# Two hybrid layers after a routed block: the first four column groups of each layer multiplied before the root is known, and four stores at the end

## The reference, cut to what matters

```python
def rmsnorm(x, w):
    xf = x.astype(jnp.float32)
    y = xf * lax.rsqrt(jnp.mean(xf * xf, axis=-1, keepdims=True) + EPS)
    return (y * w.astype(jnp.float32)).astype(x.dtype)
...
    h = rmsnorm(h_res, n_mix_pre)
    proj = jnp.einsum('bld,de->ble', h, w_in)
    (a_b, a_c, a_x, s_z, s_xbc, s_dt, r_q, r_k, r_v, r_g,
     sb_q, sb_k, sb_v, gate_logits) = jnp.split(proj, IN_SPLITS_2, axis=-1)
...
    mix = jnp.einsum('bld,de->ble', merged, w_out)
    h_res = h_res + rmsnorm(mix, n_mix_post)
    f = jnp.einsum('bld,df->blf', rmsnorm(h_res, n_ffn_pre), w_ffn_in)
    f_gate, f_up = jnp.split(f, 2, axis=-1)
    f = jnp.einsum('blf,fd->bld', jax.nn.silu(f_gate) * f_up, w_ffn_out)
    return h_res + rmsnorm(f, n_ffn_post)
```

## Time and profile before

| | us |
|---|---|
| median of three runs | 2256.66 (2256.37 to 2258.24) |
| the profiled execution | 2259.11 |
| its span in the profile | 2257.3 |
| TensorE busy | 2177.1 (96%) |
| VectorE busy | 1524.3 (68%) |
| ScalarE busy | 1186.3 (53%) |
| mean granted TensorE clock | 0.983 of full speed |

### The profile page before, as it was taken

The page is one execution under the profiler, slowest core; times in us unless marked ns, Lnnn a source line. Parts: engine busy times, 40 slices in busy tenths (PEclk is TensorE's granted clock), DMA queues, the critical chain, the costliest instruction groups (busy, mean ns, idle before and its releaser), DMA issues.

```text
span 2257.3 us, 39324 instructions
## 1 busy us (share of the span) xinstructions
PE 2177.1 (96%) x17046; PEld 2043.1 (91%) x17046; DVE 1524.3 (68%) x1923; ACT 1186.3 (53%) x1419; POOL 0.2 (0%) x4
## 2 busy tenths in 40 slices
PE   7988999999899999999998999899999999999997
PEld 6878888888899899999998999799899999998997
DVE  8977899999686675444555764786675445556763
ACT  4554677777452644436755444453644446745442
POOL 0000000000000000000000000000000000000000
PEclk9998999999999999999999999999999999999999
DMA  8473899998344444344343444345444444344552
GB/s 346 175 267 118 315 370 374 373 368 324 153 167 172 169 160 167 139 148 150 113 143 136 170 167 151 150 168 176 165 167 169 150 151 148 113 154 156 185 187 85
DMA packets 64317, 432.14 MB, mean 191 GB/s; under 512 B 7792, under 2 KB 11024, under 8 KB 13712
## 3 DMA queue, kind: packets, MB, share of 16 engines
q1 hardware_dynamic: 64144, 429.61, 51.8%
HBM read 428.50 MB, written 1.08 MB: 190 GB/s over the span
## 4 chain that ended last, share of the span: by engine, by line
PE 91%; DVE 5%; ACT 2%; issue 1%; DMA 1%; SPq 0%; ACTq 0%; DVEq 0%
PE banks L1870 64%; PE banks L1888 10%; PE quad L1888 5%; PE quad L555 1%; PE single L568 1%; PE quad L519 1%; PE quad L455 1%; DVE area_y L2386 1%; PE quad L558 1%; PE quad L503 1%; DVE slot_rounded L1005 1%; PE quad L543 1%; DVE slot_rounded L2420 1%; ACT area_y_rounded L661 1%; PE single L1562 0%
## 5 line engine op out<-in xcount | busy, mean ns | idle before, releaser
L1870 PE MATMUL banks<-spare_rounded,slot_rounded 128*128 128x272 f32 (+1 forms) x2176 | 624.2, 287 | 0.0
L1870 PE MATMUL banks<-spare_rounded,area_y_rounded 128*128 128x272 f32 (+1 forms) x1504 | 438.6, 292 | 14.3 <-DVE hn_rounded L994 12.3
L1870 PE MATMUL banks<-area_x_rounded,slot_rounded 128*128 128x272 f32 (+1 forms) x1568 | 446.7, 285 | 0.0
L1870 PE MATMUL banks<-hn_rounded,area_y_rounded 128*128 128x272 f32 (+1 forms) x1504 | 431.7, 287 | 0.0
L1870 PEld LDWEIGHTS banks<-spare_rounded,slot_rounded 128*128 128x128 f32 x2176 | 412.7, 190 | 0.0
L1005 DVE TENSOR_TENSOR slot_rounded<-slot,area_y_rounded 128x2048 fp32r<-128x2048 f32 x118 | 269.8, 2289 | 176.7 <-ACT area_y_rounded L661 176.6
L1870 PEld LDWEIGHTS banks<-spare_rounded,area_y_rounded 128*128 128x128 f32 x1504 | 285.9, 190 | 16.7 <-DVE hn_rounded L994 13.2
L1870 PEld LDWEIGHTS banks<-area_x_rounded,slot_rounded 128*128 128x128 f32 x1568 | 296.8, 189 | 0.0
L1870 PEld LDWEIGHTS banks<-hn_rounded,area_y_rounded 128*128 128x128 f32 x1504 | 285.4, 190 | 0.1
L661 ACT ACTIVATE area_y_rounded<-slot 128x2048 fp32r<-128x2048 f32 x118 | 223.7, 1906 | 32.8 <-PE banks L1870 32.8
L1005 DVE TENSOR_TENSOR slot_rounded<-slot,area_x_rounded 128x2048 fp32r<-128x2048 f32 x52 | 119.2, 2293 | 106.4 <-ACT area_x_rounded L661 106.3
(11 more groups left out here) (541 smaller groups left out, 5002.8 us busy)
## 6 DMA issues: line engine op xcount, KB each, us to landing
slot<-in_units_second SPq DMA_DIRECT2D x236, 1024.0 KB, 4.8
slot<-in_units_moe SPq DMA_DIRECT2D x100, 1024.0 KB, 4.9
slot<-in_units_first SPq DMA_DIRECT2D x32, 1024.0 KB, 6.2
spare<-in_units_moe SPq DMA_DIRECT2D x20, 1024.0 KB, 5.0
spare<-in_units_first SPq DMA_DIRECT2D x6, 1024.0 KB, 5.2
slot<-in_units_second SPq DMA_DIRECT2D x8, 768.0 KB, 4.1
merged<-acs_rows SPq DMA_DIRECT2D x4, 544.0 KB, 4.9
slot<-in_units_first SPq DMA_DIRECT2D x2, 576.0 KB, 4.2
```

The lines of the kernel that those rows point to most:

```text
L1870: ins = nc.tensor.matmul(out, weights[w], x[a], start=start and i == 0, stop=stop and i == 2, **kw)
```

## The change

Four edits. First, in each layer x0 to x3 are multiplied with the **raw** input (stream times weight, not divided by its root). ScalarE makes its high part with a copy whose scale is the weight, VectorE its low part (`raw_input_low`), pair by pair behind each residual pair; TensorE's sums of squares stand between the raw tile pairs. VectorE reads x0 to x3 out of their banks and multiplies by the root there (`scale_raw`, L1050 of the changed kernel) in place of ScalarE's copies. The divided input is still made for all other groups (`input_whole`, `input_low`). Second, unit 0 of a layer is split into high and low part in the stage before (`first_unit_high`, `first_unit_low`), for which the five slots for weights are counted through both layers. Third, the weights of the norms behind the mixer and the feed-forward part are multiplied in by ScalarE's copy out of PSUM, and `scale_mix` multiplies by the root alone, two tiles in one operation. Fourth, the result is stored in four transfers, one for each residual pair. Beside these, the experts' last sums use other PSUM banks.

```diff
+RAW_UNITS = 2
...
-            self.xbc += hop(2, "act")
+            self.xbc += hop(2, "act" if n >= RAW_UNITS else "dve")
...
-        self.slot = {u: (u % LAYER_SLOTS, u // LAYER_SLOTS + 1) for u in range(len(self.units))}
+    def slot(self, L, unit):
+
+        return (L * len(self.units) + unit) % LAYER_SLOTS
+
+    def landed(self, L, unit):
+
...
-    stream_total(0, slice(0, T))
-    hn = (m.hn_high, m.hn_low)
-
-
-    together(plan.xbc[:2], hn, s.input_low)
-    for g in plan.inner[2:]:
+    hn, raw = (m.hn_high, m.hn_low), (m.raw_high, m.raw_low)
+
+    def raw_tiles(pair):
+
+        pe.wait_ge(s.raw_low.sem, s.raw_low.at(L, pair + 1))
+        for g in plan.xbc[:2]:
+            if pair == 0:
+                ready(g)
+            multiply(g, raw, (2 * pair, 2 * pair + 1))
+
+    def raw_squares(pair):
+
+        pe.wait_ge(s.stream_squared.sem, s.stream_squared.at(L, pair + 1))
+        for t in (2 * pair, 2 * pair + 1):
+            ins = add_squares(t, slice(0, T))
+        return ins
+
+    for pair in range(KT // 2 - 1):
+        raw_tiles(pair)
+        raw_squares(pair)
+    tick(raw_squares(KT // 2 - 1), s.stat)
+    raw_tiles(KT // 2 - 1)
+    for g in plan.xbc[2:2 * RAW_UNITS]:
+        group(g, raw)
+    together(plan.z[:2], [part[:, :, Q] for part in hn], s.input_low)
+    for g in plan.inner[2 * RAW_UNITS + 2:]:
         group(g)
     pe.wait_ge(s.dt_weights.sem, s.dt_weights.at(L, 1))
...
+def first_unit_high(act, nc, m, s, plan, L):
+
+    slot = plan.slot(L, 0)
+    act.wait_ge(m.landed[slot].sem, m.landed[slot].at(0, plan.landed(L, 0)))
+    nc.scalar.activation(m.mixer_high[0], m.slots[slot][:, :], ACT.Copy).then_inc(s.mix_high.sem, 1)
+    s.mix_high.n += 1
+
+
+def first_unit_low(v, nc, m, s, plan, L):
+
+    slot = plan.slot(L, 0)
+    v.wait_ge(s.mix_high.sem, s.mix_high.at(L, 1))
+    nc.vector.tensor_tensor(m.slots_low[slot][:, :], m.slots[slot][:, :], m.mixer_high[0].bitcast(F32), ALU.subtract).then_inc(s.mix_low.sem, 1)
+    s.mix_low.n += 1
+
+
+def raw_input_low(own, v, nc, m, s, L, pair):
+
+    gain = PAR_AT["norm_mix_pre"][0]
+    v.wait_ge(s.raw_high.sem, s.raw_high.at(L, pair + 1))
+    for k in (2 * pair, 2 * pair + 1):
+        ins = nc.vector.scalar_tensor_tensor(m.raw_low[:, k, :], m.h[:, k, :], m.par_all[:, L, gain + k:gain + k + 1], m.raw_high[:, k, :].bitcast(F32),
+                                             ALU.mult, ALU.subtract)
+        own.tick(ins, s.raw_low if k % 2 else s.dve_step)
+
+
 def second_scalar(act, nc, m, s, plan, L):
...
-    stream_squares(-KT // 2, slice(0, T))
-    mixer_highs = []
+    gain = L * PAR + PAR_AT["norm_mix_pre"][0]
+    gains = m.par_all.rearrange("p l n -> p (l n)")
+    for pair in range(KT // 2):
+        act.wait_ge(s.residual.sem, s.residual.at(L, -KT // 2 + pair + 1))
+        for k in (2 * pair, 2 * pair + 1):
+            tick(f(m.raw_high[:, k, :], m.h[:, k, :], ACT.Copy, scale=gains[:, gain + k:gain + k + 1]), s.raw_high if k % 2 else s.act_step)
+        both = slice(2 * pair, 2 * pair + 2)
+        tick(f(m.th[:, both, :], m.h[:, both, :], ACT.Square), s.stream_squared)
+    mixer_highs = [plan.mixer_split[0]]
...
     for pair in range(KT // 2):
         act.wait_ge(s.input_whole.sem, s.input_whole.at(L, pair + 1))
-        tick(f(m.hn_high[:, 2 * pair:2 * pair + 2, :], m.hn[:, 2 * pair:2 * pair + 2, :], ACT.Copy), s.input_high)
+        tick(f(m.hn_high[:, 2 * pair:2 * pair + 2, :], m.th[:, 2 * pair:2 * pair + 2, :], ACT.Copy), s.input_high)
...
-            tick(f(m.cpad[:, j % 4, SSD_K - 1:SSD_K - 1 + T], bank(g), ACT.Copy), s.act_free)
+            if g.freer == "act":
+                tick(f(m.cpad[:, j % 4, SSD_K - 1:SSD_K - 1 + T], bank(g), ACT.Copy), s.act_free)
...
-            tick(f(w.mix[:, t, :], bank(g), ACT.Copy), s.act_free)
+            tick(f(w.mix[:, t, :], bank(g), ACT.Copy, scale=m.par[:, at + t:at + t + 1]), s.act_free)
...
+        if p == 2 and L + 1 < LAYERS:
+            first_unit_high(act, nc, m, s, plan, L + 1)
...
+    def scale_raw(j):
+
+        g = plan.xbc[j]
+        done(g)
+        tick(tt(m.cpad[:, j % 4, SSD_K - 1:SSD_K - 1 + T], bank(g), m.root[:, :], ALU.mult), s.dve_free)
+
+    def input_whole(pair):
+
+        for k in (2 * pair, 2 * pair + 1):
+            tick(stt(m.th[:, k, :], m.h[:, k, :], par("norm_mix_pre", k), m.root[:, :], ALU.mult, ALU.mult), s.input_whole if k % 2 else s.dve_step)
+
+    def input_low(pair):
+
+        both = slice(2 * pair, 2 * pair + 2)
+        v.wait_ge(s.input_high.sem, s.input_high.at(L, pair + 1))
+        tick(tt(m.hn_low[:, both, :], m.th[:, both, :], m.hn_high[:, both, :].bitcast(F32), ALU.subtract), s.input_low)
+
...
-    rms_norm(1, "norm_mix_pre", s.input_whole, s.input_high, m.hn_high, s.input_low, m.hn_low)
+    v.wait_ge(s.std.sem, s.std.at(L, 1))
+    input_whole(0)
+    scale_raw(0)
+    scale_raw(1)
+    input_whole(1)
+    v.wait_ge(s.gemm.sem, s.gemm.at(L, plan.last_use[0] + 1))
+    input_low(0)
+    input_whole(2)
+    input_low(1)
+    scale_raw(2)
+    input_whole(3)
+    input_low(2)
+    input_low(3)
     mixer_low()
-    mixer_low()
+    scale_raw(3)
 
     def conv(j):
-        v.wait_ge(s.act_free.sem, s.act_free.at(L, plan.xbc[j].freed))
+        if plan.xbc[j].freer == "act":
...
-    def scale_mix(pair, gain):
-        for t in (2 * pair, 2 * pair + 1):
-            tick(stt(w.mix[:, t, :], w.mix[:, t, :], par(gain, t), m.root[:, Q], ALU.mult, ALU.mult), s.dve_step)
+    def scale_mix(pair):
+        both = w.mix[:, 2 * pair:2 * pair + 2, :]
+        tick(tt(both, both, m.root[:, Q].unsqueeze(1).to_broadcast([128, 2, T - q0]), ALU.mult), s.dve_step)
...
-    add_widths(1, range(1, KT - 1))
+    add_widths(1, range(1, KT - 2))
+    if L + 1 < LAYERS:
+        first_unit_low(v, nc, m, s, plan, L + 1)
+    add_widths(1, range(KT - 2, KT - 1))
     v.wait_ge(s.std.sem, s.std.at(L, 6))
     v.wait_ge(s.act_free.sem, s.act_free.at(L, plan.down[-1][2][1].freed))
     for pair in range(KT // 2):
-        scale_mix(pair, "norm_ffn_post")
+        scale_mix(pair)
         settle()
         add_mix(pair)
-    settle()
-
-
-ACT_STEPS, DVE_STEPS = 78, 206
+        if pair and L + 1 < LAYERS:
+            raw_input_low(own, v, nc, m, s, L + 1, pair - 1)
...
-            sp.wait_ge(s.gemm.sem, s.gemm.at(L, plan.last_use[u - LAYER_SLOTS] + 1))
+        slot, behind = plan.slot(L, u), L * len(plan.units) + u - LAYER_SLOTS
+        if behind >= 0:
+            sp.wait_ge(s.gemm.sem, s.gemm.at(behind // len(plan.units), plan.last_use[behind % len(plan.units)] + 1))
         else:
...
+        if t == KT - 2:
+            pe.wait_ge(s.turned_low.sem, PAIRS)
...
+    first_unit_high(act, nc, m, s, plan, 0)
...
+    first_unit_low(v, nc, m, s, plan, 0)
...
+        if t % 2 and t > 1:
+            raw_input_low(own, v, nc, m, s, 0, t // 2 - 1)
+    raw_input_low(own, v, nc, m, s, 0, KT // 2 - 1)
...
+        m.mixer_high[0] = hn_rounded[:, 0:UNIT]
+        m.raw_high, m.raw_low = Area(yb_rounded).cut(KT, T), Area(ya_rounded).cut(KT, T)
...
-        m.scatter_bank = lambda i: (m.quad[:, 1024:1536], m.quad[:, 1536:2048], m.gemm[0], m.gemm[1])[i]
+        m.scatter_bank = lambda i: (m.single[:, :], m.quad[:, 1024:1536], m.quad[:, 1536:2048], m.gemm[2])[i]
...
-            sp.wait_ge(s.residual.sem, s.residual.at(LAYERS, 0))
-            sp.dma_start(out, m.h[:, :, META:T]).then_inc(stored, 16)
-            sp.wait_ge(stored, 16)
+            for pair in range(KT // 2):
+                both = slice(2 * pair, 2 * pair + 2)
+                sp.wait_ge(s.residual.sem, s.residual.at(LAYERS - 1, KT // 2 + pair + 1))
+                sp.dma_start(out[:, both, :], m.h[:, both, META:T]).then_inc(stored, 16)
```

More of the change, by code:

```diff
@@ L315, in multiply @@
     def multiply(g, x, tiles):
-        slot = plan.slot[g.unit][0]
-        low = m.slots_low[slot]
+        low = m.slots_low[plan.slot(L, g.unit)]
         if g.unit in plan.mixer_split:
@@ L896, in second_scalar, with widths @@
             tick(f(w.merged_high[:, t - 1:t + 1, :], w.merged[:, t - 1:t + 1, :], ACT.Copy), s.merged_high)
-    def widths(groups, first=0):
+    def widths(groups, first, gain):
+        at = PAR_AT[gain][0]
         for t, g in enumerate(groups, first):
@@ L982, in second_vector @@
     tick(tt(m.dt_low, w_dt, m.dt_high.bitcast(F32), ALU.subtract), s.dt_weights)
[L984 to L996 removed]
+    def scale_raw(j):
[9 more added lines that the diff above has]
+        tick(tt(m.hn_low[:, both, :], m.th[:, both, :], m.hn_high[:, both, :].bitcast(F32), ALU.subtract), s.input_low)
+    mixer_lows = [plan.mixer_split[0]]
     def mixer_low():
@@ L1310, in second_vector @@
     for pair in range(KT // 2):
-        scale_mix(pair, "norm_mix_post")
+        scale_mix(pair)
         settle()
```

58 lines of the change are left out of this document (24 added, 34 removed).

## The result

The changed kernel takes 2260.70 us (median of 22 runs, 2257.61 to 2263.68), the kernel before, timed beside it, 2256.56 (22 runs, 2254.75 to 2258.66). The ratio is 1.0019, with a 95% interval of 1.0014 to 1.0025: slower by 4.1 us, at the edge of what tells a change from none. The forecast was 2258.8.

What follows compares the result with a forecast made beforehand. TensorE, busy 96% of the span, was taken as the bound, with VectorE only about 1.0 us ahead at x5. Terms 0.85 + 1.5 + 3.4 - 0.8 - 2.8 = +2.15 on 2256.66 gave 2258.8 us, range 2248.0 to 2262.5.

Steps and rivals of the forecast that it cites:

- Root and c0: Layer 0: root 5.0 us later; c0, where VectorE's list up to z0's read-out starts, 9.9 us behind the root.
- x5 terms: Later start of x5 through the later c0: +0.85 us in layer 0, +1.5 us (0.8 to 2.2) in layer 1.
- c0 + 13.8: When z0's bank, which x5 needs, is free: VectorE's fixed list from c0 takes 13.34 us.
- the groups ahead of it are no bound: Before x5: z0 and x4 get the low parts of units 2 and 3 in time, so they set no limit.
- The clock behind x5: TensorE pauses some 3.5 us before x5, then runs at low clock: 1.7 us per layer, +3.4 us, bounds 0 and 6.2.
- long-stretch rival: Restarts before x5 stay at low clock 6.2 us, not 3.4, and layer 1's raw part too: 2262.3 us; chance 0.15.
- Layer 1's slow raw part: TensorE's raw products in layer 1 run at half speed after a 4.8 us pause, costing 2.4 us (1.7 to 3.1).
- Feed-forward starts: Two scale_mix ahead of the first low part, each 0.2 us shorter: -0.8 us for both layers.
- The end: Four shorter residual pairs (0.76 us) and a last store of 256 KB landing after 2.7 us: -2.8 us (-3.0 to -0.8).
- What was said to cost nothing: First unit's early split (1.9 us ScalarE, 2.3 VectorE) hides under TensorE's products; its weights, turned_low wait and PSUM banks cost nothing.

Runs made afterwards that it cites:

- e1: Changed kernel, with ScalarE loading the table for tanh right behind the rounding of the input in both layers; 2256.77 us, ratio 1.0002 to the kernel before.
- e2: Changed kernel plus 17 matmuls of ones, result not read, between x4 and x5 in each layer; 2256.38 us, ratio 1.0001 to the kernel before.
- e4: Kernel before plus only the norms' weights multiplied in ScalarE's copy, one scale_mix for two tiles, and four stores; 2252.6 us, ratio 0.9971.

## Why the prediction was right, and where it wasn't

The time lies in the range, and the forecast's main statement held: the removed wait comes back before x5, because VectorE had 1.0 us of room and reaches c0 later. That the median is only 1.9 us above the forecast is in part luck: the terms for the table load and for the clock were short by 2.7 and 2.3 us in the profiles, and a larger gain at the end and 2.9 us of other differences, most of them of the clock, made up for over half of it.

- *Root and c0.* The root was to end 5.0 us later, counted from the first residual addition, and did within 0.2; c0 was to come 9.9 us behind it and came at 9.86 in both layers. The part of the x5 terms that follows from it measured +1.00 in layer 0 (forecast 0.85) and +1.23 in layer 1 (forecast 1.5).
- *"c0 + 13.8" for x5: the step that failed.* I took VectorE's list from c0 to z0's read-out as fixed at 13.34 us, since it had no gap in it before. It measured 14.70, because one entry, the low part of unit 3, hangs on ScalarE, and ScalarE's table load had moved behind a wait. A term of +2.7 is missing from the sum, and e1 shows it. The prediction did not follow ScalarE's own waits from the rounding to the first tanh. For the same reason *"the groups ahead of it are no bound"* failed for x4, which waited 0.56 and 0.90 us for unit 3's low part; that cost nothing, since x5 waits anyway.
- *The clock behind x5: mis-sized.* Forecast 1.7 per layer, measured 2.9. I had taken low stretches of 3.4 us from two of three rows; the restarts brought 6.8, as the third row had it. Here the long-stretch rival's mechanism came true. e2 shows the term: filling the pause returns 4.3. In each layer one long pause before x0 has become two, before z0 and before x5, and each has a low stretch behind it. The Trainium skill ("TensorE: Matmul & The Clock Gate", HAM oscillation) has it that pauses which come again and again throttle the array anew each time; the trace agrees for these four. It isn't so for every pause: behind the one of 1.98 us in layer 1 the clock held (1.00 from 1612).
- *Layer 1's slow raw part.* 2.4 forecast; the slow matmuls run from 1431.62 to 1436.52, 4.9 us at half speed, so 2.45.
- *Feed-forward starts* -0.8 forecast, -0.75 measured. *The end* -2.8 and -3.26: the last store landed in 2.1 us, not 2.7. e4 gives the two small parts together 4.0 by medians (3.8 to 9.3 by the interval), against 3.6 forecast.
- *What was said to cost nothing* did: no wait in the list after the change names the early split of the first unit.

The sum of the corrected terms is +6.6 in the profiles, and the medians differ by 4.1. In the profiles 2.9 us stand against it, most of them differences of the clock. Whether these hold over all runs isn't known: e1 and e2 returned 3.9 and 4.3 us in medians, with intervals of 2 us to either side, so the medians can't divide the change more finely than that.
